# The bias term of a long convolution put into the filter's first tap, and its back tables issued ahead of a wait

## The reference, cut to what matters

```python
def bidirectional_long_conv(u, h_fwd, h_bwd):
    L = u.shape[1]
    k = jnp.concatenate([h_fwd, jnp.zeros_like(h_fwd[:1]), h_bwd[:0:-1]], axis=0)
    k = k / jnp.sum(jnp.abs(k), axis=0, keepdims=True)
    k_f = jnp.fft.rfft(k, n=2 * L, axis=0)
    u_f = jnp.fft.rfft(u, n=2 * L, axis=1)
    return jnp.fft.irfft(u_f * k_f[None], n=2 * L, axis=1)[:, :L]

def hyena_mixer(u, ...):
    ...
    z = x1 * v
    z = bidirectional_long_conv(z, h_fwd, h_bwd) + z * f_bias.astype(jnp.float32)
    return x0 * z
```

## Time and profile before

| | us |
|---|---|
| three runs | 2594.49, 2596.62, 2596.85 |
| their median | 2596.62 |
| the profiled execution | 2594.16 |
| its span, from the first to the last instruction | 2592.4 |
| `transform_mixes` in it | about 226 to 387 |

### The profile page before, as it was taken

The page is one execution under the profiler, slowest core; times in us unless marked ns, Lnnn a source line. Parts: engine busy times, 40 slices in busy tenths (PEclk is TensorE's granted clock), DMA queues, the critical chain, the costliest instruction groups (busy, mean ns, idle before and its releaser), DMA issues. The chain is left out here.

```text
span 2592.4 us, 28506 instructions
## 1 busy us (share of the span) xinstructions
PE 2414.8 (93%) x11168; PEld 1829.9 (71%) x11168; DVE 1580.5 (61%) x1700; ACT 1064.0 (41%) x1281; POOL 411.2 (16%) x284
## 2 busy tenths in 40 slices
PE   7999988949999999975999999998969999999998
PEld 6776554836666666655776778887858888887787
DVE  5552665357999999968212652223589998874444
ACT  4221103226777777755213641112344344433322
POOL 3110301011222222210300210000032333210000
PEclk9999998969999999997999999999989999999999
DMA  5121032269999999976310011113212222226343
GB/s 160 41 67 53 17 103 96 82 275 332 380 375 385 378 363 378 375 263 229 115 49 17 2 32 46 49 49 150 74 49 81 90 82 90 79 81 227 122 159 138
DMA packets 192965, 397.27 MB, mean 153 GB/s; under 512 B 17270, under 2 KB 120694, under 8 KB 176456
## 3 DMA queue, kind: packets, MB, share of 16 engines
q1 hardware_dynamic: 183624, 378.76, 41.2%
q0 software_dynamic: 9216, 16.80, 2.1%
HBM read 357.75 MB, written 47.18 MB: 156 GB/s over the span
## 5 line engine op out<-in xcount | busy, mean ns | idle before, releaser
L1398 DVE TENSOR_TENSOR expert_rest<-expert_raw,expert_high 128x2048 fp32r<-128x2048 f32 x135 | 306.1, 2290 | 43.7 <-ACT expert_high L1392 41.7
L1392 ACT ACTIVATE expert_high<-expert_raw 128x2048 fp32r<-128x2048 f32 x135 | 258.0, 1913 | 24.4 <-PE expert_up_ps L143 8.5
L141 PE MATMUL up_ps<-blocks_high,up_operand_high 128*128 128x512 f32 x616 | 241.5, 392 | 15.0 <-DVE plain_blocks_rest L3013 11.7
L143 PE MATMUL up_ps<-blocks_high,up_operand_rest 128*128 128x512 f32 x616 | 240.7, 391 | 0.0
L1805 POOL DMA_INDIRECT expert_rows<-y_rows,out_ids x32 | 84.5, 2639 | 425.2 <-DVE y_rows L1759 425.2
L141 PE MATMUL down_ps<-w_down_high,prod_high 128*128 128x512 f32 x352 | 138.2, 393 | 8.1 <-DVE w_down_rest L185 8.1
L141 PEld LDWEIGHTS up_ps<-blocks_high,up_operand_high 128*128 128x128 f32 x616 | 116.3, 189 | 41.0 <-issue 16.8
L3230 DVE TENSOR_TENSOR up_operand_rest<-res,up_operand_high 128x512 fp32r<-128x512 f32 x154 | 143.1, 940 | 3.0 <-ACT up_operand_high L3186 3.0
L1398 DVE TENSOR_TENSOR expert_rest<-res,expert_high 128x2048 fp32r<-128x2048 f32 x57 | 129.6, 2290 | 15.0 <-ACT expert_high L1392 14.4
L142 PE MATMUL down_ps<-w_down_rest,prod_high 128*128 128x512 f32 x352 | 137.7, 391 | 0.0
L142 PE MATMUL up_ps<-plain_blocks_rest,up_operand_high 128*128 128x512 f32 x352 | 137.6, 391 | 0.0
(11 more groups left out here) (432 smaller groups left out, 5944.1 us busy)
## 6 DMA issues: line engine op xcount, KB each, us to landing
expert_raw<-in_w_down_dram SPq DMA_DIRECT2D x46, 1024.0 KB, 19.1
expert_raw<-in_w_up_dram SPq DMA_DIRECT2D x45, 1024.0 KB, 19.4
expert_raw<-in_w_gate_dram SPq DMA_DIRECT2D x44, 1024.0 KB, 17.4
res<-in_w_up_dram SPq DMA_DIRECT2D x88, 256.0 KB, 3.9
res<-in_w_down_dram SPq DMA_DIRECT2D x44, 512.0 KB, 4.1
res<-in_w_gate_dram SPq DMA_DIRECT2D x20, 1024.0 KB, 22.0
res<-in_w_in_dram SPq DMA_DIRECT2D x38, 512.0 KB, 4.4
res<-in_w_up_dram SPq DMA_DIRECT2D x19, 1024.0 KB, 20.2
```

Source lines behind the costliest of these rows:

```text
L141: nc.tensor.matmul(out, w_high, x_high, start=start, stop=False)
L143: return nc.tensor.matmul(out, w_rest, x_high, start=False, stop=stop)
L1392: self.nc.scalar.activation(self.high_part[:, n % SPLIT_SLOTS, :], self.raw[n % RAW_SLOTS], ACT.Copy) \
L1398: self.nc.vector.tensor_tensor(self.rest_part[:, s, :], self.raw[n % RAW_SLOTS], self.high_part[:, s, :].bitcast(F32), ALU.subtract).then_ ...
```

## The change

The bias term moves from the signal to the filter. TensorE makes four small products behind the transposes, which turn the four columns of `bias_size` into one row of 512 channels in bank 7 (`bias_turned`). VectorE adds this row to row 0 of `lag_sum` and of `lag_dif`, ahead of all its other work in the block (`bias_done` counts 2 now), and TensorE waits for both ahead of the second group of forward products, which writes bank 7. GpSimd's four products and TensorE's 16 identity products go, with their waits; the first back product into each bank opens its sum instead.

The output weights' loads, and the wait for `v_done` 2, move from behind the third back table to behind the seventh (`BACK + 6`): the fourth to the seventh table are issued ahead of the wait. Two loads go with the last two tables and the other six follow.

```diff
--- before.py
+++ after.py
@@ -671,6 +671,7 @@
         mid_kept = sem("mid_kept")
         v_done = sem("v_done")
         four_kept = sem("four_kept")
+        bias_turned = sem("bias_turned")
         bias_done = sem("bias_done")
         steps = Steps(sem("mix_steps"))
         DFT, BACK, N_TILES = 2 * JT, 4 * JT, 6 * JT
@@ -704,14 +705,14 @@
                 if n >= SLOTS:
                     sp.wait_ge(tab_used, n - SLOTS + 1)
                 sp.dma_start(place(n), table_tile(n)).then_inc(tab_in[n % SLOTS], 16)
-                if n >= BACK + 2:
-
-                    if n == BACK + 2:
+                if n >= BACK + 6:
+
+                    if n == BACK + 6:
                         sp.wait_ge(v_done, 2)
-                    load_w_out(sp, n - (BACK + 2))
+                    load_w_out(sp, n - (BACK + 6))
                 if n == 1:
                     sp.dma_start(pair[:], A["pair_table"].rearrange("p t c -> p (t c)")).then_inc(pair_in, 16)
-            for k in range(N_TILES - (BACK + 2), KT):
+            for k in range(N_TILES - (BACK + 6), KT):
                 load_w_out(sp, k)
 
         @block.tensor
@@ -765,8 +766,14 @@
                     last = nc.tensor.transpose(ps[:, n % 4, c * P:(c + 1) * P],
                                                m.zT[:, c, at:BANK * (n % 2 + 1):4], m.ident[:])
                 last.then_inc(z_turned, 1)
+            for c in range(HT):
+                last = nc.tensor.matmul(ps[0:1, 7, c * P:(c + 1) * P], m.bias_size[:, c:c + 1], m.ident[:],
+                                        start=True, stop=True)
+            last.then_inc(bias_turned, 1)
             pe.wait_ge(z_kept, 2 * JT)
             for g in range(4):
+                if g == 1:
+                    pe.wait_ge(bias_done, 2)
                 if g >= 2:
                     pe.wait_ge(split_done, g - 1)
                 for a in range(2):
@@ -810,11 +817,6 @@
                                                     stop=(a == 1 and trig == 1))
                         last.then_inc(tab_used, 1)
             pe.wait_ge(four_kept, 2 * HT + 1)
-            pe.wait_ge(bias_done, HT)
-            for c in range(HT):
-                for par in range(2):
-                    nc.tensor.matmul(ps[:, 2 * c + par, :].rearrange("p (s i) -> p s i", s=2), m.ident[:], of_parity(m.zT, c, par),
-                                     start=True, stop=False)
             for f in range(2):
                 pe.wait_ge(v_done, f + 1)
                 for par in range(2):
@@ -826,7 +828,7 @@
                                 last = nc.tensor.matmul(ps[:, 2 * c + par, phase * QUART:(phase + 1) * QUART],
                                                         V[:, trig, par + 2 * phase, f, c * P:(c + 1) * P],
                                                         table[:, n % SLOTS, phase:HALF:2],
-                                                        start=False,
+                                                        start=(f == 0 and trig == 0 and phase == 0),
                                                         stop=(f == 1 and trig == 1 and phase == 1))
                         last.then_inc(tab_used, 1)
 
@@ -889,13 +891,11 @@
                                                given[:, :, SEQ - 1:HALF:-2], op)
             last.then_inc(fold_done, 1)
 
-            pool.wait_ge(z_turned, 2 * JT)
-            for c in range(HT):
-                nc.gpsimd.tensor_scalar(m.zT[:, c, :], m.zT[:, c, :], m.bias_size[:, c:c + 1], None, ALU.mult) \
-                    .then_inc(bias_done, 1)
-
         @block.vector
         def _(dve):
+            dve.wait_ge(bias_turned, 1)
+            for lags in (lag_sum, lag_dif):
+                nc.vector.tensor_tensor(lags[0:1, 0, :], lags[0:1, 0, :], ps[0:1, 7, :], ALU.add).then_inc(bias_done, 1)
             for g in range(4):
                 par, trig = g // 2, g % 2
                 dve.wait_ge(later_kept, g + 1)
```

## The result

| | us |
|---|---|
| before, five runs: median (least to most) | 2595.33 (2594.49 to 2596.85) |
| after, five runs: median (least to most) | 2581.84 (2580.04 to 2583.05) |
| ratio, 95% interval | 0.9947 [0.9936, 0.9958] |
| profiled execution of after | 2580.04, of which 2578.2 span |

The kernel is 0.53% faster, 13.5 us between the medians and 14.2 us between the spans (2592.4 against 2578.2). The forecast was 2582.2, in a range of 2577 to 2588. Measured once more later (the last experiment), the gain between the medians is 12.5 us.

A forecast was written before the change was run, and what follows sets the result against it. TensorE, busy 93% of the span, was taken as the bound. The median of 2596.62 us less 14.4 for the identity products, every other term taken as nothing, gave 2582.2, range 2577 to 2588.

The forecast's parts named there:

- What bounds: Whole program: TensorE busy 93% of the span, so a shorter TensorE stage shortens the whole by as much.
- Identity products: Between Fourier and back products: removing 16 of them gains 14.2 to 14.5 us, taken as 14.4.
- V's second half: Middle of the back products: spare 0.75 us, cost nothing; rival that it is late, 2583.6 us, chance 0.06.
- Tables and weights: Loads around the back products: cost nothing; rivals fourth table late, 2588.1 us, chance 0.03, and weights' loads, 2586, chance 0.04.
- Bias products: Behind the transposes: four added products, 0.5 us, hidden in TensorE's 0.75 us stand; 0.5 with that cover gone.
- The adds on one row: Head of VectorE's program: two adds of 0.85 us each, between 0.485 and 1.22, spare over 4 us, cost nothing.
- GpSimd's products: Four products in 11.31 us from 283.99, removed with TensorE's wait for them: gain nothing.
- The clock: Scatter around 2.7 us; rival: half clock from the 2 us gap through the back products, 2611 us, chance 0.03.

The follow-up runs named there:

- the last experiment: The changed kernel measured once more with no edit: 2582.90 us against 2595.36 before, ratio 0.9947.
- the run with the late weights: Changed kernel with all eight output weights' loads put behind the use of the last back table: 2591.46 us against 2596.05 before, ratio 0.9983.
- the loads alone: The kernel before with only the new order of loads, identity products kept: 2594.92 us against 2596.05, ratio 0.9998.
- the run with GpSimd's adds: Changed kernel with back products in another order of channel groups and four of V's adds on GpSimd: 2583.99 us against 2595.69 before, ratio 0.9950.

## Why the prediction was right

- **What bounds.** That TensorE's time in the stage is the program's time held: 14.25 us shorter in the stage, 14.2 in the span, 13.5 in the medians (12.5 when measured once more). The rest of the program took 2204.7 us against 2204.8. Over the other profiles it lies between 2205.2 and 2208.1 with the same code behind the stage (the run with the late weights apart), so single spans can differ by 3 us without a cause in the change; this is the scatter that the prediction had taken as 2.7 to 3.
- **How near the time came.** That 2581.84 lies within 0.4 us of the forecast is in part luck. The prediction started from a median of 2596.62 of three runs, which is 2595.33 with five, 1.3 lower; and the gain is 13.5 where 14.4 was taken, 0.9 less. The two errors nearly cancel. The chances as listed also add up to 0.95 for faster and 0.02 for the same, not to the 0.94 and 0.03 given.
- **Identity products.** 14.4 was taken; the back products start 1.97 us behind the Fourier products, as the identity products did, and the term is 14.47 less 0.08.
- **V's second half.** Forecast 0.75 us of spare, 0.83 in the profile; made late by 7 us it opens a gap of 6.27, and with TensorE 2 us earlier one of 0.89. VectorE's products (L934) take 4.63 us at 339.31, beside the back products, so they run there as beside the Fourier products.
- **Tables and weights.** The forecast order of issues came to within 0.5 us: first weights at 353.56 (forecast 353.28), table 8 at 354.54 (354.0), the other weights from 354.91. These seven took longer than forecast: the last, issued at 358.72, landed 10.1 us later, at 368.85 instead of 366, which cost nothing as the first weights are read at 375.92. That the table's place matters is shown from both sides: with the old order the gain falls by 8.6 us, and the new order alone gives nothing.
- **Bias products.** This term was mis-sized: 0.5 us for four products were 1.03 us for eight rows, since an fp32 product has two rows and I had priced each as one row. They outgrow the cover of 0.75, and 0.14 us come onto the path, where the prediction took nothing and gave 0.5 as the bound with the cover gone; the bound itself was too low, as the doubled products cost 0.87.
- **The adds on one row.** 0.64 us each, in the range of 0.485 to 1.22, hidden as said.
- **GpSimd's products.** Nothing, as said: no instruction of VectorE ran beside them with two operands in SBUF.
- **The clock.** The prediction had it as a scatter without a cause in the change, and as a rival in which the half clock stays down through all of the back products. Neither is quite what happens. Behind the gap of 2 us the clock comes down in some executions, for a few us, and this costs the back products 1.6 us; the identity products behind the same gap lost nothing. So the change has made the stage sensitive to it: its gain is 14.2 us in an execution without the dip and about 12.6 in one with it. A granted clock under 1.00 in the back products was one of the prediction's own signs of being wrong: the first profile of the changed kernel does not show it, the second does. How often the dip falls there, and what decides it, is left open; of the eight profiles with this gap (before and the loads alone among them) it is in three, and of the three in which other products fill the gap in none, which is too few to show that the gap causes it.

## What to carry to other kernels

Work that is taken off the engine that bounds a stage is worth its whole length only as far as the next thing is in time: list what the old work was covering (here a load held behind another load's wait, and the second half of an operand), and move that along in the same change. Count a product by the rows that the trace has for products of its type, not by the lines of code. A short stand ahead of dense products costs more than its length when the clock drops behind it. Filling it with products that need nothing of what is waited for (other banks first) takes the stand away; whether it takes that risk away too is not shown, though no dip came there in the three profiles with it filled.

## What the runs showed of the hardware

- With gaps of TensorE the clock fell to 0.50 for some us. In the gaps of 5.5 and 6.3 us it fell while TensorE stood (1.6 and 2.8 us lost in the products behind); in the gap of 2.8 us, in the run with GpSimd's adds, it was still 1.00 and fell after the products had begun (64 rows in 16.36 instead of 14.77 us); and behind the same 1.97 us it fell in three executions and not in five. The Trainium skill (TensorE: Matmul & The Clock Gate, Part 1: The HAM clock gate) says that the gate's observation runs free of the kernel's start, so that the place of a change differs between runs; two profiles of one program that differ at one gap agree with that.
- The identity products, whose moving operand is read with a stride (0.90 us a row of 512 columns against 0.43), took the same 14.64 us with the clock at 0.53 to 0.62 over four of them as at 1.00 throughout, so what limits them is not TensorE's clock. That it is the stride is not shown: no run has the same products without it.
- With VectorE and GpSimd each adding or multiplying two operands from SBUF, VectorE was slowed: its four products from 4.63 to 7.83 us. GpSimd probably was too: its add of 512 columns took 2.25 us, where its product of 512 columns in the next stage takes 1.02 (2.04 for two); no run has the same adds without VectorE beside them.
